# Rows for the experts stored unnormalised, a down matrix loaded with the others, and tables moved

## The reference

```python
h = rmsnorm(x, norm_ffn_g[l])               # x * rsqrt(mean(x*x) + EPS) * g, by token
group_prob = softmax(h @ rg_w + rg_b)       # 4 groups
gate = p_grp * softmax(top_val)             # two experts of a group for each token
xs = xt[slot_tok].reshape(n_blocks, MOE_BLOCK, D)
a = xb @ w_gate[e]                          # 1024 x 512
u = xb @ w_up[e]                            # 1024 x 512
y = (silu(a) * u) @ w_down[e]               # 512 x 1024
out = zeros.at[slot_tok].add(y * slot_gate)
```

## Time and profile before

| | us |
|---|---|
| median of three runs | 2002.62 |
| lowest and highest run | 1997.75, 2004.81 |
| profiled execution: its time | 1999.79 |
| profiled execution: its span | 1998.3 |
| TensorE busy | 1833.8 (92%) |
| VectorE busy | 848.2 (42%) |
| GpSimd busy | 1049.0 (52%) |
| ScalarE busy | 442.0 (22%) |

### The profile page before, as it was taken

How to read it: one execution, slowest core, us unless ns; L and a number is a source line. 1 busy time by engine, 2 the same in 40 slices (tenths; PEclk the granted TensorE clock), 3 DMA queues, 4 the chain that set the end, 5 groups by cost and what they waited for, 6 DMA issues and landing times.

```text
span 1998.3 us, 27813 instructions
## 1 busy us (share of the span) xinstructions
PE 1833.8 (92%) x9860; PEld 1280.8 (64%) x9860; DVE 848.2 (42%) x1317; ACT 442.0 (22%) x813; POOL 1049.0 (52%) x642
## 2 busy tenths in 40 slices
PE   7999999999999899999999979998968978869788
PEld 6888888887776678888888756765743333323333
DVE  6444434320344577444443389777351211111113
ACT  3111100100344432111100143552321211111112
POOL 7888888777544378888887533321212222222222
PEclk9999999999999899999999989999979988988889
DMA  4333353432211123333332212210578999999996
GB/s 161 95 94 95 107 180 101 139 102 86 64 55 52 37 90 95 95 95 98 101 106 92 88 42 74 67 61 22 204 302 350 372 405 392 408 409 386 413 398 250
DMA packets 54340, 338.88 MB, mean 170 GB/s; under 512 B 8266, under 2 KB 8650, under 8 KB 42256
## 3 DMA queue, kind: packets, MB, share of 16 engines
q1 hardware_dynamic: 45792, 319.31, 44.1%
q0 software_dynamic: 5712, 10.71, 1.6%
q10 hardware_dynamic: 2784, 8.19, 1.1%
HBM read 475.06 MB, written 15.09 MB: 245 GB/s over the span
## 4 chain that ended last, share of the span: by engine, by line
PE 72%; DMA 13%; DVE 9%; ACT 3%; issue 1%; POOL 1%; SPq 0%; DVEq 0%; ACTq 0%; POOLq 0%
PE bank L486 31%; PE bank L457 12%; DMA big<-w_up_in 11%; PE bank L1882 7%; PE bank L740 4%; PE bank L1366 4%; DVE big L1092 2%; PE bank L1900 2%; PE bank L505 2%; PE bank L1480 2%; DMA ring<-w_down_in 1%; PE bank L1908 1%; PE bank L658 1%; DVE state L1077 1%; PE bank L718 1%
## 5 line engine op out<-in xcount | busy, mean ns | idle before, releaser
L299 POOL TENSOR_TENSOR weights_hi_parts<-ring,ones 128x1024 fp32r<-128x1024 f32 (+1 forms) x174 | 352.1, 2023 | 281.0 <-PE bank L486 120.1
L301 POOL TENSOR_TENSOR ring_parts<-ring,weights_hi_parts 128x1024 fp32r<-128x1024 f32 (+1 forms) x174 | 468.3, 2691 | 13.7
L486 PE MATMUL bank<-attention_buffers_parts,weights_hi_parts 128*128 128x512 f32 x832 | 325.9, 392 | 11.5 <-POOL small L235 10.2
L486 PE MATMUL bank<-state_parts,weights_hi_parts 128*128 128x512 f32 x832 | 324.7, 390 | 0.0
L486 PE MATMUL bank<-attention_buffers_parts,ring_parts 128*128 128x512 f32 x832 | 324.5, 390 | 0.0
L1882 PE MATMUL bank<-big,work 128*32 128x512 f32 x1440 | 226.5, 674 | 51.8 <-DMA big<-w_up_in 51.8
L457 PE MATMUL bank<-big_parts,weights_hi_parts 128*128 128x512 f32 x704 | 217.0, 389 | 1.2 <-POOL ring_parts L301 1.2
L912 POOL TENSOR_TENSOR ring_parts<-ring,weights_hi_parts 128x1024 fp32r<-128x1024 f32 x32 | 80.7, 2523 | 222.6 <-ACT weights_hi_parts L909 222.6
L486 PEld LDWEIGHTS bank<-attention_buffers_parts,weights_hi_parts 128*128 128x128 f32 x832 | 156.7, 188 | 45.4 <-POOL small L235 10.1
L486 PEld LDWEIGHTS bank<-state_parts,weights_hi_parts 128*128 128x128 f32 x832 | 156.7, 188 | 33.0 <-issue 0.5
L486 PEld LDWEIGHTS bank<-attention_buffers_parts,ring_parts 128*128 128x128 f32 x832 | 156.7, 188 | 32.6
(11 more groups left out here) (418 smaller groups left out, 2929.5 us busy)
## 6 DMA issues: line engine op xcount, KB each, us to landing
big<-w_up_in SPq DMA_DIRECT2D x54, 2048.0 KB
ring<-wdense_in SPq DMA_DIRECT2D x176, 512.0 KB, 3.6
state<-w_down_in SPq DMA_DIRECT2D x37, 2048.0 KB
big<-w_gate_in SPq DMA_DIRECT2D x36, 2048.0 KB
attention_buffers<-w_gate_in SPq DMA_DIRECT2D x18, 2048.0 KB
ring<-w_down_in SPq DMA_DIRECT2D x18, 2048.0 KB
ring<-wff_in SPq DMA_DIRECT2D x32, 704.0 KB, 4.1
results_by_token<-big ACTq DMA_DIRECT2D x1, 4096.0 KB, 15.4
```

Source lines behind the costliest of these rows:

```text
L299: po.tensor_tensor(hi, raw, ones[:, 0:1].to_broadcast([128, words]), ALU.mult).then_inc(PO.sem, 1)
L301: po.tensor_tensor(lo, raw, hi.bitcast(F32), ALU.subtract) \
L486: m = pe.matmul(out, x, y_, start=j + n == 0, stop=j == len(pairs) - 1 and n == len(ts) - 1)
```

## The change

1. GpSimd stores the rows of `x_tok` as VectorE's copies leave them. The four multiplications by the root on ScalarE are gone, and the stores wait for `out_copied` in place of them.
2. The root goes into the gate and up products when they are evicted: `row_scale` now holds root (gate products) or root times gate (up products). For that VectorE makes one more table, `oh_root`, and one more product of four values a partition; the selection by `is_up` and `not_up` becomes a plain copy, and five operations of GpSimd at the program's start that made these two are gone.
3. The down matrix of set 2 is started with the three of the second group, ahead of the final gain. Its wait is for steps of ScalarE and VectorE that read `nrm`.
4. The operations for the gates stand behind the first block's rows (`keep_rows`, `take_rows`) on VectorE, and count in a semaphore of their own.

```diff
-    half_row, last_row, is_up, not_up = sm(1), sm(1), sm(1), sm(1)
+    half_row, last_row, not_up = sm(1), sm(1), sm(1)
...
     load_expert(1, 2, 2)
+    for done in (split_u[3], spread_read[0], *silus.values(), *split.values()):
+        sp.wait_ge(done.queue.sem, done.value(None))
+    load_expert(2, 2, 2)
     sp.dma_start(final_gain, rows_d[:, ROWS["final2"]:ROWS["final2"] + D]).then_inc(s_gain, 16)
...
     s = DV.run(dv.reciprocal(st[:, 0:4], st[:, 0:4]))
-    AC.wait(s)
-    h_tok = nrm
+    token_root = s
     for t in range(NT):
-        PO.wait(AC.step(ac.activation(h_tok[:, t * D:(t + 1) * D], x_tok[:, t * D:(t + 1) * D], ACT.Identity,
-                                      scale=st[:, t:t + 1])))
-        po.dma_start(h_d[t * 128:(t + 1) * 128, :], h_tok[:, t * D:(t + 1) * D]).then_inc(s_hrow, 16)
+        PO.wait(out_copied[0][t], out_copied[1][t])
+        po.dma_start(h_d[t * 128:(t + 1) * 128, :], x_tok[:, t * D:(t + 1) * D]).then_inc(s_hrow, 16)
 
     sp.wait_ge(PE.sem, PE.n)
     sp.wait_ge(s_gath[0], 16)
     load_expert(2, 1, 1)
-    load_expert(2, 2, 2)
...
-    def by_rows(bank, cols_, table, copies):
+    def by_rows(bank, cols_, tables_):
...
-            for g in range(copies):
+            for g, table in enumerate(tables_):
...
     row_scale = sm(SLOT_COLS)
+    DG = Queue("dg", nc.vector, sem("gate_tables"))
+    DG.wait(gexp, exp2)
+    DG.run(dv.tensor_reduce(gsum, gex3, axis=AX.X, op=ALU.add))
+    DG.run(dv.scalar_tensor_tensor(gsum, e2, 1.0, gsum, ALU.add, ALU.mult))
+    DG.run(dv.reciprocal(gates[:, 0:NT], gsum))
+    DG.run(dv.tensor_tensor(gates[:, 0:NT], gates[:, 0:NT], st[:, 0:4], ALU.mult))
+    DG.run(dv.tensor_tensor(gates[:, NT:2 * NT], gates[:, 0:NT], e2, ALU.mult))
+    oh_root = oh_tok
+    DG.step(dv.tensor_tensor(by_slot(oh_gate), by_slot(oh_slot), over_last(gates, C2, SLOT_COLS), ALU.mult))
...
+    gated_slots = DG.step(dv.tensor_tensor(oh_root.rearrange("p (j t n) -> p j t n", j=2, t=NT),
+                                           oh_slot.rearrange("p (j t n) -> p j t n", j=2, t=NT), tok_roots, ALU.mult))
     dv.wait_ge(s_spread, 1)
-    dv.tensor_scalar(row_scale, banks[7][:, 0:SLOT_COLS], is_up, not_up, ALU.mult, ALU.add).then_inc(DV.sem, 3)
+    dv.tensor_copy(row_scale, banks[7][:, 0:SLOT_COLS]).then_inc(DV.sem, 3)
...
-    by_rows(banks[7], slice(0, SLOT_COLS), oh_gate, 4).then_inc(s_spread, 1)
+    by_rows(banks[7], slice(0, SLOT_COLS), (oh_root, oh_gate, oh_root, oh_gate)).then_inc(s_spread, 1)
```

More of the change, by code:

```diff
@@ L239, in build @@
     PO.run(po.tensor_tensor(last_row, last_row, half_row, ALU.add))
-    PO.run(po.tensor_scalar(is_up, tok_id[:, 0:1], float(3 * BS - NO_ROW), None, ALU.is_ge))
-    PO.run(po.tensor_scalar(not_up, tok_id[:, 0:1], float(2 * BS - NO_ROW), None, ALU.is_ge))
-    PO.run(po.tensor_tensor(is_up, is_up, half_row, ALU.add))
-    PO.run(po.tensor_tensor(is_up, is_up, not_up, ALU.subtract))
-    PO.run(po.tensor_scalar(not_up, is_up, -1.0, 1.0, ALU.mult, ALU.add))
     numbered = PO.run(po.tensor_scalar(half_row, half_row, float(2 * NO_ROW), None, ALU.add))
@@ L1005, in build @@
     v2_ready, rows_ready, sig_read, stats_read = [], [], [selectors], {}
-    floored = {}
+    floored, spread_read = {}, []
     next_taps, x_ready, own_taps, diagonals, tap_at = [], [], {}, [], {}
@@ L1321, in conv_norm @@
             split_u[k] = split_chunk(chunk(ym, k), chunk(ym_parts.hi, k), chunk(ym_parts.lo, k), s)
+            spread_read[0:] = [split_u[k]]
             est("ac", 0.7)
@@ L1760, in by_rows @@
         return m
-    s = PE.step(by_rows(banks[2], slice(0, SLOT_COLS), oh_tok, 2))
+    s = PE.step(by_rows(banks[2], slice(0, SLOT_COLS), (oh_tok, oh_tok)))
     DV.run(dv.scalar_tensor_tensor(ids1, rmod, 0.0, ids1, ALU.is_equal, ALU.mult))
@@ L1816, in build @@
     DV.step(dv.tensor_scalar(added_to.bitcast(I32), row_at, last_row[0:2 * BS, :], None, ALU.min))
-    DV.wait(gexp)
-    DV.run(dv.tensor_reduce(gsum, gex3, axis=AX.X, op=ALU.add))
-    DV.wait(exp2)
-    DV.run(dv.scalar_tensor_tensor(gsum, e2, 1.0, gsum, ALU.add, ALU.mult))
-    DV.run(dv.reciprocal(gates[:, 0:NT], gsum))
-    DV.run(dv.tensor_tensor(gates[:, NT:2 * NT], gates[:, 0:NT], e2, ALU.mult))
-    gated_slots = DV.run(dv.tensor_tensor(by_slot(oh_gate), by_slot(oh_slot), over_last(gates, C2, SLOT_COLS), ALU.mult))
     exp1, exp_i, need = sm(SLOT_COLS), sm(SLOT_COLS), sm(SLOT_COLS)
@@ L1849, in build @@
     row_scale = sm(SLOT_COLS)
+    DG = Queue("dg", nc.vector, sem("gate_tables"))
[7 more added lines that the diff above has]
+    DG.step(dv.tensor_tensor(by_slot(oh_gate), by_slot(oh_slot), over_last(gates, C2, SLOT_COLS), ALU.mult))
+    tok_roots = st[:, 0:4].unsqueeze(1).to_broadcast([128, 2, NT]).unsqueeze(3).to_broadcast([128, 2, NT, SLOT_COLS])
+    gated_slots = DG.step(dv.tensor_tensor(oh_root.rearrange("p (j t n) -> p j t n", j=2, t=NT),
+                                           oh_slot.rearrange("p (j t n) -> p j t n", j=2, t=NT), tok_roots, ALU.mult))
     dv.wait_ge(s_spread, 1)
-    dv.tensor_scalar(row_scale, banks[7][:, 0:SLOT_COLS], is_up, not_up, ALU.mult, ALU.add).then_inc(DV.sem, 3)
+    dv.tensor_copy(row_scale, banks[7][:, 0:SLOT_COLS]).then_inc(DV.sem, 3)
     DV.n += 5
```

## The result

The changed kernel's median is 1999.12 us (1995.04 to 2000.78, 12 runs), beside 2002.86 us (1997.75 to 2007.19, 12 runs) for the kernel before: the medians differ by 3.7 us, or 0.19%. The ratio that is given with the runs is 0.9978, with a 95% interval from 0.9970 to 0.9986, which is 4.4 us, from 2.8 to 6.0. So the kernel is faster, but by less than the 0.3% that the prediction counts as faster. The forecast was 1998.9 us. The profiled execution took 1995.04 us with a span of 1993.8, 4.5 us less than before.

The account below looks back on a forecast made before the run. The block loop was taken as bound by DMA of expert matrices, TensorE waiting for them. Gain 4.7 less gather delay 1.0 gave 3.7 us: execution 1996.1, median 1998.9 us, range 1994.0 to 2003.5.

Parts of the forecast that it names:

- The moved down matrix: At the first gather: one down matrix less in the stream behind 1480 us, gain 4.7 us, 4.1 to 5.2.
- the sum: Whole kernel: 4.7 us gained less 1.0 us of gather delay gives 3.7 us.
- TensorE has to follow: From 1495 to 1527 us: TensorE's 5.6 us of waits let it follow the earlier stream by up to 5.6 us.
- head start lost: Rival, 1534 to 1552 us: TensorE cannot follow, as when its clock falls; gain 0, 2002.6 us, chance 0.22.
- One step of the working: Ahead of block 3's gate matrix: remaining down matrix through at about 1488.2, queue empty up to 0.8 us, 0.4 taken.
- The gather's delay: First gather, 1477.41 us: early stores share engines with four matrices and land late, cost 1.0 us, between 0 and 2.8.
- no delay: Rival, first gather: the stores land before 1477.41 us; gain 4.7 to 5.2 us, 1997.7 us, chance 0.28.
- The edits costed at nothing: ScalarE's multiplications, gates' operations, GpSimd's five operations at the start: gain 0; `row_scale` copy: 0, at most 0.1 us.
- The signs: Changed profile: no empty stretch before about 1476 us, gather 1477.4 to 1480, q0 18 to 21 packets a us, 0.99 from about 1550.
- The shift at 1490 found at 1960: Expert loop: the shift at 1490 us must be found at 1960 us, or the prediction is wrong.
- Slower: Rival, first gather: stores land last, at 1482.1 us, 4.7 late, and gathers take longer; 4.1 us slower, 2006.7 us, chance 0.08.

Follow-up runs that it names:

- e1_load_back: Changed kernel with the down matrix of set 2 started behind the first gather again, all other edits kept: 2003.49 us, ratio 0.9997.
- e2_gates_first: Changed kernel with the gates' operations put back ahead of the experts' tables on VectorE: 1999.31 us, ratio 0.9977.
- e5_five_ops: Changed kernel with GpSimd's five small operations at the start put back, results unused: 1998.72 us, ratio 0.9984.
- e8_later_stores: Changed kernel with the row stores held until ScalarE's first exponential, early down matrix kept: 1998.89 us, ratio 0.9985.
- e9_after_again: The changed kernel itself, unaltered, run again on the same chip as two kernels with added products: 1998.29 us.
- e4_no_gather_wait: Changed kernel without SyncE's wait for the first gather, so the last of the first nine matrices loads before it: 1999.74 us, ratio 0.9989.
- e12_second_no_wait: Changed kernel with 8 added unread TensorE products and no first-gather wait for the last of the first nine matrices: 1997.93 us, ratio 0.9980.
- e3_late_stores: Changed kernel with the stores, still of unnormalised rows, held until the token's root is known: 1999.87 us, ratio 0.9986.
- e10_warm_second: Changed kernel with 8 added unread TensorE products, 6 behind the experts' order and 2 ahead of the gather's wait: 1994.95 us, ratio 0.9965.

## Why the prediction was right, and where it was not

**The moved down matrix (4.7 us, 4.1 to 5.2): mechanism right, size too large by the time it reached the loop.** At matrix 9 the term is as forecast: 15.2 - 9.9 = 5.3 us in the two profiles, and 14.95 - 9.94 = 5.0 as means (before and `e1_load_back` against after, `e2_gates_first`, `e5_five_ops`, `e8_later_stores`, `e9_after_again`). At matrix 15 the same means give 53.75 - 49.58 = 4.2, with 48.2 to 50.2 for the five profiles of the second. The term of the sum that was mis-sized is this one, by "TensorE has to follow": the sum carried the full 4.7 through. From 1495 to 1527 TensorE's waits fell only from 5.6 to 3.1 us and the DMA share from 1.00 to 0.88. The stream was ahead, and the issue at 1527.88 came into an empty queue; from 1527 to 1554 before, and from 1523 to 1550 after, TensorE waits for nothing. So there the handover is TensorE's. How much of the shift arrives then hangs on TensorE's clock just ahead of it. From matrix 12 to matrix 15, in after and in `e9_after_again`, the same program:

```profile
1505.28:1528.85 23.57, 20.44 (x176) 8.19 (x172) 3.83 (x15) 3.81 (x7) 5.66 (x11) 0.93 0.77 290
```

```profile
1508.63:1530.19 21.56, 19.13 (x176) 7.76 (x180) 4.16 (x15) 4.08 (x8) 5.68 (x11) 1.00 0.82 315
```

In after TensorE stood idle for 1.6 us until 1519.4, for a down matrix, and ran at 0.50 from 1520 to 1523; in `e9_after_again` it was idle for 1.3 us, until 1522.4, and kept 1.00. `e2_gates_first`, `e5_five_ops` and `e8_later_stores` are like after (0.93, 23.2 to 23.3 us). In `e9_after_again`, where the clock stayed up, matrix 15 comes 48.2 us behind the gather, 5.5 us sooner than the mean of 53.75: the whole shift arrives. In before the clock had fallen as well (0.92, 22.3 us). So the 1 us that was given back is a mean over four profiles with such a fall and one without, which fits the mechanism that the rival "head start lost" named; with one profile on the other side it isn't shown to be the whole cause. What decides whether the clock falls there no run shows. The medians of `e4_no_gather_wait` and `e12_second_no_wait` fit the same limit with another matrix.

One step of the working was also off by itself: 2.10 MB from 1481.4 at 334 GB/s end at 1487.7, not at 1488.2, which would leave 1.3 us empty and not 0.8. The trace shows no empty queue: the first packet of matrix 9 starts at 1488.55, while the last ones of the down matrix end at 1489.55.

**The gather's delay (1.0 us, 0 to 2.8): too large, it is 0, the lower end.** The 18 packets a us of the earlier trace rows were read as a limit of the store's queue when both move. With four matrices it was 64 packets in the same three microseconds, 21.3 a us, and 453 GB/s in all. Over its whole length the store took 1452.3 to 1475.3 for 512 packets, 22.3 a us; the forecast had 18 to 20.9. Beside them 417 rows of 16 KB moved, 412 GB/s in all. The rival "no delay" had this term right, and with it the estimate of 20.9 turns a us that the prediction took from the Trainium skill ("DMA: Bandwidth & Descriptors", section "Queues, rings and completion order"), which was nearer than mine and still a little low; by that estimate nothing was late, so it didn't speak against the edit, as the prediction has it. The stores at 1458.26 in `e3_late_stores` show that the delay was possible: it is there at once, 1.1 us, when they start 8 us later.

**The sum.** 4.2 - 0 is within 0.5 us of 4.7 - 1.0 = 3.7: two misses of opposite sign cancelled in part. That the median of 1999.12 sits 0.2 us from the forecast is luck beyond that, with 2.8 to 6.0 us left open by the interval, and it isn't a proof of the working. The profiled pair shows 4.0 us from matrix 4 to matrix 92 (509.7 before, 505.7 after); the other 0.5 us of its 4.5 were there before the change's place, and `e5_five_ops` shows that no edit made them.

**The edits costed at nothing.** GpSimd's five operations: 0, shown by `e5_five_ops`. The gates' operations: 0 within 0.4 us, shown by `e2_gates_first`; their new place ends them 3.3 us before TensorE needs them, where the prediction had 2.4 of cover. ScalarE's four multiplications and the scaled rows in the stores: nothing of the time came back in `e1_load_back`, where they stay removed. Their removal isn't idle all the same: the scaled rows lay in the very buffer (`state`) that the moved down matrix fills at 1448.50, so without storing the rows unscaled the load could not have gone early. What the prediction listed as free edits are the condition of the one that pays. `row_scale`'s copy stands 0.15 us earlier than in the earlier trace rows, while the work around it is 0.5 us earlier: it starts 1.65 us behind the end of the first product instead of 1.28, and no run tells the cause.

**The signs.** The group without an empty stretch (0.99 to 1474), 2.5 us empty before the gather, the gather before 1480, one down matrix, the gate matrix 7.65 us behind it (7.5 forecast), 0.99 from 1550: as written. Not as written: the gather at 1476.93 lies ahead of the 1477.4 to 1480 of the forecast, by as much as the whole group was early; the store's queue moved 22.3 packets a us, not 18 to 21; and 3.1 us of TensorE's waits are left where 5.6 less 4.2 would be 1.4. The first product took 5.52 us (1481.53 to 1487.05), 0.02 over the 5.5 that the prediction set as a sign of being wrong; before it took 5.46, so that sign was set too close to tell anything. "The shift at 1490 found at 1960" holds for 4.5 of 5.8 us (matrix 9 at 1488.5 instead of 1494.3, matrix 92 at 1953.5 instead of 1958.0), which is the first point again.

**The rivals.** "Head start lost" decided nothing as a whole, but its place was right, and in small perhaps its mechanism: the stretch that belongs to TensorE, with its clock down for 3 us, took about 1 of 5 us. "Slower" needed stores that land after 1482.1; their last packet started at 1475.3.

## What to carry to other kernels

A transfer moved into an empty stretch is worth its own length only up to the next handover that compute sets; look for the first stretch behind it in which the engine waits for nothing, and count the engine's waits ahead of it as the most that can be gained. Here they were 5.6 us, the transfer gave 5.0, and 4.2 arrived as a mean, with the engine's clock down behind one of the waits that were left in four of five profiles. When several transfers share a queue group and something waits for one of them, ask for the end of the group's bytes and not for its own issue time: issued 0.3, 8.4 or 15.0 us into the group, the stores ended at 27.5, 28.8 and 28.6. And compare by distances within one profile, from one packet to another, when executions differ by more than the change gives.

## What the runs showed of the hardware

The granted clock goes with a good part of what executions of this kernel differ by. Over the 33, 35, 20 and 17 executions of the kernel before that ran beside the experiments, the mean granted clock and the time have correlations of -0.79, -0.72, -0.87 and -0.72. TensorE is busy all through the stretch before routing, and in 7 of 14 profiles its clock fell already there. Of after, then of `e10_warm_second`:

```profile
1450.00:1456.00 6.00, 5.71 (x51) 5.36 (x50) 1.86 (x6) 3.59 (x10) 0.44 (x1) 1.00 1.02 423
```

```profile
1450.00:1456.00 6.00, 6.00 (x37) 5.77 (x36) 1.00 (x2) 2.35 (x7) 1.40 (x3) 0.62 0.95 393
```

Where it does, the gather comes 2.7 to 3.3 us later behind matrix 4. Another such fall, of `e9_after_again`, stands where this second profile of the same program falls back: from matrix 0, the first of the expert matrices, to matrix 4 it takes 29.8 us instead of 26.9, which is 2.9 of the 3.3 us by which its group starts later:

```profile
1430.00:1441.00 11.00, 11.00 (x40) 8.79 (x39) 2.48 (x4) 3.79 (x9) 4.66 (x2) 0.77 1.00 429
```

And two queues together need not be slower than one. The 333 GB/s of the earlier trace rows were taken for the price of small packets beside large ones; with the same mixture, at the same place, it was 453 GB/s after, and 412 GB/s over the whole store, where loads alone had 429 in the earlier trace rows. Nor is it that the store's queue had only just begun, as the prediction put it. In its first three microseconds twelve of the fourteen profiles moved 398 to 435 GB/s. Only before (337) and `e8_later_stores` were slow; of `e8_later_stores`, then of after:

```profile
1467.78:1470.78 3.00, 2.25 (x10) 1.98 (x9) 2.62 (x16) 0.00 (x0) 0.00 (x0) 0.50 0.92 332
```

```profile
1452.34:1455.34 3.00, 2.96 (x29) 2.85 (x27) 0.88 (x3) 1.52 (x5) 0.00 (x0) 1.00 1.00 416
```

These two are the ones in which the store's first packet came 4 to 5 us before the end of the group's last matrix (1461.70 of 1466.65, 1467.78 of 1472.00). Why the end of a group should be slow was not tried.
